# Two transformer blocks on one core: the second block's gates from un-normed tiles, its last two HGRN levels from buffers of their own

## What is computed

```python
x = rmsnorm(x_lat, final_norm)                    # end of block one
xn = rmsnorm_2(x, norm_mix)                       # start of block two
proj = xn @ w_in + b_in                           # h_q, h_f_fwd, h_f_bwd, h_i, h_g, m_q, m_k, m_v, m_o, 16 gates
q_h = silu(h_q);  lf = log_sigmoid(h_f) per direction;  k = 1 - exp(lf)
# HGRN2 per head and direction:  S_t = diag(f_t) S_{t-1} + k_t v_t^T,  o_t = S_t^T q_t
```

## Time and profile before

| | us |
|---|---|
| median of 3 runs | 1798.23 |
| lowest, highest | 1798.11, 1799.66 |
| profiled execution | 1801.54 |
| its span, first to last instruction | 1799.8 |
| PE busy | 1711.2 |
| VectorE busy | 959.0 |
| ScalarE busy | 702.5 |
| GpSimd busy | 138.6 |

### The profile page before, as it was taken

The page is one execution under the profiler, slowest core; times in us unless marked ns, Lnnn a source line. Parts: engine busy times, 40 slices in busy tenths (PEclk is TensorE's granted clock), DMA queues, the critical chain, the costliest instruction groups (busy, mean ns, idle before and its releaser), DMA issues.

```text
span 1799.8 us, 18749 instructions
## 1 busy us (share of the span) xinstructions
PE 1711.2 (95%) x7182; PEld 1289.3 (72%) x7182; DVE 959.0 (53%) x1325; ACT 702.5 (39%) x1024; POOL 138.6 (8%) x150
## 2 busy tenths in 40 slices
PE   7999988989999999999898998989998999999997
PEld 1478755355788888888687877558875688888886
DVE  5867576265454433442568779575533353434343
ACT  2631354312344312334464556865433331313141
POOL 0312000014300000003000000213000100000001
PEclk9999999999999999999899999999999999999999
DMA  9334113401313224213232121334311213232221
GB/s 325 109 116 164 59 48 106 174 37 47 94 48 102 94 86 138 95 59 105 103 119 81 47 59 36 110 121 164 128 59 47 90 53 107 107 106 99 93 93 47
DMA packets 113237, 174.43 MB, mean 97 GB/s; under 512 B 3788, under 2 KB 56524, under 8 KB 112717
## 3 DMA queue, kind: packets, MB, share of 16 engines
q1 hardware_dynamic: 109404, 160.76, 26.2%
q0 software_dynamic: 3760, 12.72, 2.2%
HBM read 169.00 MB, written 4.46 MB: 96 GB/s over the span
## 4 chain that ended last, share of the span: by engine, by line
PE 82%; DVE 7%; ACT 5%; issue 3%; DMA 1%; POOL 1%; SPq 0%; DVEq 0%; ACTq 0%; POOLq 0%
PE bank L833 15%; PE bank L834 15%; PE bank L835 15%; PE bank L866 6%; PE bank L867 6%; PE bank L871 5%; PE bank L891 3%; PE bank L1077 2%; PE bank L940 2%; PE bank L1090 1%; PE bank L1020 1%; PE bank L1032 1%; PE bank L1357 1%; PE bank L1388 1%; PE bank L1207 1%
## 5 line engine op out<-in xcount | busy, mean ns | idle before, releaser
L2945 POOL TENSOR_TENSOR arena<-arena 128x512 f32<-128x512 f32 (+1 forms) x56 | 74.1, 1329 | 981.4 <-ACT arena L1483 977.6
L835 PE MATMUL bank<-hx_hi,weight_slots_lo 128*128 128x512 f32 x320 | 125.7, 393 | 0.0
L1452 ACT ACTIVATE weights_hi<-weight_slots 128x2048 fp32r<-128x2048 f32 (+2 forms) x46 | 77.0, 1725 | 122.2 <-DMA weight_slots<-in_ffn_w_down 65.4
L2089 ACT ACTIVATE weights_hi<-weight_slots 128x2048 fp32r<-128x2048 f32 x30 | 55.8, 1909 | 162.9 <-DMA weight_slots<-in_w_up 108.7
L2902 DVE TENSOR_TENSOR weight_slots_lo<-weight_slots,weights_hi 128x2048 fp32r<-128x2048 f32 x30 | 67.4, 2288 | 87.1 <-ACT weights_hi L2089 87.1
L834 PE MATMUL bank<-xn_lo,weights_hi 128*128 128x512 f32 x288 | 112.0, 389 | 0.0
L1438 ACT ACTIVATE arena<-bank 128x512 f32<-128x512 f32 (+3 forms) x110 | 54.8, 537 | 138.0 <-PE bank L835 50.4
L833 PE MATMUL bank<-sq_hi,weights_hi 128*128 128x512 f32 x256 | 99.6, 389 | 0.0
L834 PE MATMUL bank<-sq_lo,weights_hi 128*128 128x512 f32 x256 | 99.6, 389 | 0.0
L835 PE MATMUL bank<-sq_hi,weight_slots_lo 128*128 128x512 f32 x256 | 99.6, 389 | 0.0
L2139 DVE TENSOR_TENSOR weight_slots_lo<-weight_slots,weights_hi 128x2048 fp32r<-128x2048 f32 (+2 forms) x36 | 70.2, 1990 | 29.8 <-ACT weights_hi L1452 29.8
(11 more groups left out here) (422 smaller groups left out, 4138.4 us busy)
## 6 DMA issues: line engine op xcount, KB each, us to landing
weight_slots<-in_w_in SPq DMA_DIRECT2D x24, 1024.0 KB, 7.0
weight_slots<-in_ffn_w_up SPq DMA_DIRECT2D x22, 1024.0 KB, 6.5
weight_slots<-in_w_up SPq DMA_DIRECT2D x16, 1024.0 KB, 6.5
weight_slots<-in_w_down SPq DMA_DIRECT2D x16, 1024.0 KB, 6.3
weight_slots<-in_w_mod SPq DMA_DIRECT2D x14, 1024.0 KB, 7.7
arena<-in_w_mod POOLq DMA_DIRECT2D x32, 256.0 KB, 3.3
weight_slots<-in_w_out SPq DMA_DIRECT2D x8, 1024.0 KB, 7.6
weight_slots<-in_w_xkv SPq DMA_DIRECT2D x8, 1024.0 KB, 7.4
```

What stands on the lines that cost most here:

```text
L835: return mm(ps, ll, rh, start=False, stop=stop)
L1452: A(high_half(kind, n, i), W[:, s_, a:b], ACT.Copy).then_inc(w_hi, 1)
L2089: A(W_hi[:, s % 2, a:b], W[:, s % 2, a:b], ACT.Copy).then_inc(w_hi, 1)
L2945: G.tensor_tensor(acc, acc, sq[i % 2][:, 0:width], ALU.add).then_inc(sq_added, 1)
```

## The change

1. **Un-normed gates and hq.** ScalarE copies xg_hi = x * gain_mix2 right behind each tile's squares, and VectorE makes xg_lo (`gained_low`). PE does the gate and hq products with these; the norm sums stand between tiles k = 2 and k = 3. VectorE multiplies the five results with rstd on the way out of PSUM, then ScalarE adds biases and takes the Silu in place. hx is still made, for ff and the later projections. Slab down,7 is split by ScalarE behind the squares of three tiles, and slab in2,1 before hx's high parts; VectorE splits both halves of in2,0 before it adds up tile 7.
2. **Slab waits by halves.** Gates and hq start at half 0 of in2,0 and wait for half 1 at k = 4; hi, mv and mq (all that 3 + n < RING lets through) do the same with theirs.
3. **Work moved between the f and b projections.** Own keys of hp 0 (behind n = 6), the subtraction that makes Gc (per tile instead of over 2048 columns), x's normalising (behind n = 0 and 2; the store x_rest follows it, now behind the transfer of in2,2). The references of the far levels are made at place (1, 3); the mask cast moves behind level 2's exponents.
4. **Far exponents in ScalarE.** For levels 256 and 512, `exponents` is no longer called. ScalarE computes exp(ref - F) with the reference as its bias, in pieces of 128 columns, and the other halves in larger pieces (10 activations for 256, 14 for 512).
5. **Buffers of their own.** For hp 1 the far levels use the parts of Fc, Gc, kf and kb that belonged to hp 0 (`far_buffers`), and are made at places (4, 3) and (5, 0). The gate scans wait for (1,512)'s scores, since they write there.

```diff
+FAR_AT = {(4, 3): 256, (5, 0): 512}
+REFERENCES = (1, 3)
...
+OWN_KEYS = 6
+GAINED_LOW = {2: (0, 1), 3: (2,), 5: (3, 4), 6: (5, 6)}
+MID_TILES = {0: range(0, 4), 2: range(4, 8)}
 IN2_SPLIT = 6
 
 
-HIGH_HOMES = {3: (54, 74), 4: (58, 70), 5: (54, 50)}
+HIGH_HOMES = {1: (32, 40), 3: (54, 74), 4: (58, 70), 5: (54, 50)}
...
+        xg_hi = parts("xg_hi", 54, 8)
+        xg_lo = [parts("xg_lo_26", 26, 6)[:, k, :] for k in range(6)] + [parts("xg_lo_14", 14, 2)[:, k, :] for k in range(2)]
...
+        def far_buffers(lev):
+
+            return [t[:, 0:1024] for t in ((Fc, Gc) if lev == 256 else (kf, kb))]
+
+        def near_count(hp, lev):
+
+            return len(LEVELS) * hp + LEVELS.index(lev) + 1
...
+            slab("in2", 2, io["w_in_2"], 1024)
             sp.wait_ge(normed, sum(norms["norm_mid"]))
             sp.dma_start(x_rest, x).then_inc(sem("x_away"), 16)
-            slab("in2", 2, io["w_in_2"], 1024)
...
-            norm_sum("norm_mid")
-            norm_sum("norm_mix2")
-
             pe.wait_ge(sem("wgate_lo"), 1)
-            w = split_slab("in2", 0)
+            pe.wait_ge(w_lo, 2 * split_no["in2", 0] + 1)
+            w = [v.rearrange("p (k c) -> p k c", k=KD) for v in (high("in2", 0), low("in2", 0))]
             gates, *banks = [open_bank(name) for name in ["gates"] + [f"hq_{m}" for m in range(HC)]]
             cols = [slice(P * m, P * m + P) for m in range(HC)]
             for k in range(KD):
-
-                pe.wait_ge(x_hi, operand_no["hx", k] + 1)
-                mm(gates[:], wgate_hi[:, k, :], hx_hi[:, k, :], start=k == 0, stop=False)
-                mm(gates[:], wgate_lo[:, k, :], hx_hi[:, k, :], start=False, stop=False)
+                if k == 4:
+                    pe.wait_ge(w_lo, 2 * split_no["in2", 0] + 2)
+                if k == 3:
+                    norm_sum("norm_mid")
+                    norm_sum("norm_mix2")
+
+                pe.wait_ge(x_hi, operand_no["xg", k] + 1)
+                mm(gates[:], wgate_hi[:, k, :], xg_hi[:, k, :], start=k == 0, stop=False)
+                mm(gates[:], wgate_lo[:, k, :], xg_hi[:, k, :], start=False, stop=False)
                 for c, ps in zip(cols, banks):
-                    mm(ps[:], w[0][:, k, c], hx_hi[:, k, :], start=k == 0, stop=False)
-                    mm(ps[:], w[1][:, k, c], hx_hi[:, k, :], start=False, stop=False)
+                    mm(ps[:], w[0][:, k, c], xg_hi[:, k, :], start=k == 0, stop=False)
+                    mm(ps[:], w[1][:, k, c], xg_hi[:, k, :], start=False, stop=False)
...
+                if hp and lev > P:
+                    pe.wait_ge(sem("far_decay_A"), 1 + (lev == 512))
+                    pe.wait_ge(sem("far_B_ready"), 1 + (lev == 512))
+                    A, B = far_buffers(lev)
+                elif lev:
...
-                    pe.wait_ge(w_lo, 2 * split_no["in2", 3 + n] + 2)
+                    pe.wait_ge(w_lo, 2 * split_no["in2", 3 + n] + 1)
...
+                    if 3 + n < RING and k == KD // 2:
+                        pe.wait_ge(w_lo, 2 * split_no["in2", 3 + n] + 2)
...
+                if k == 3:
+                    split_w("down", 7)
                 evicted(act, f"down_{KD + k}")
                 square_tile("norm_mid", k, x[:, k, :])
                 square_tile("norm_mix2", k, x[:, k, :], scale=pc("final_norm", k))
+                if k == 0:
+                    act.wait_ge(sem("gain_mix2"), 1)
+                A(xg_hi[:, k, :], x[:, k, :], ACT.Copy, scale=gain_mix2[:, k:k + 1]).then_inc(x_hi, 1)
...
+            def far_exp(hp, lev, dst, left, right, dl, dr):
+
+                o, l, r = (v.rearrange("p (h j t) -> p h j t", h=2, j=NT)
+                           for v in (dst, left[:, 1024 * hp:1024 * hp + 1024], right[:, 1024 * hp:1024 * hp + 1024]))
+
+                def from_ref(h, j, row):
+                    c = 4 * (2 * hp + h) + j
+                    return A(o[:, h, j, :], l[:, h, j, :], ACT.Exp, scale=-1.0, bias=refs[:, row, c:c + 1])
...
+                if lev == 256:
+                    for h in range(2):
+                        for j in (0, 2):
+                            from_ref(h, j, dl)
+                    return A(o[:, :, 1:4:2, :], r[:, :, 1:4:2, :], ACT.Exp)
+                for h in range(2):
+                    for j in (0, 1):
+                        from_ref(h, j, dl + 2)
+                A(o[:, :, 2, :], r[:, :, 2, :], ACT.Exp)
+                for h in range(2):
+                    c = 4 * (2 * hp + h) + 2
+                    ins = A(o[:, h, 3, :], r[:, h, 3, :], ACT.Exp, bias=refs[:, dr, c:c + 1])
+                return ins
...
+                        far_exp(hp, lev, A_, kf, kb, 0, 1).then_inc(sem("far_decay_A"), 1)
+                        far_exp(hp, lev, B_, Gc, Fc, 1, 0).then_inc(sem("far_decay_B"), 1)
...
+            def gained_low(k):
+
+                dve.wait_ge(x_hi, operand_no["xg", k] + 1)
+                V.scalar_tensor_tensor(xg_lo[k], x[:, k, :], gain_mix2[:, k:k + 1], xg_hi[:, k, :].bitcast(F32),
+                                       ALU.mult, ALU.subtract).then_inc(x_lo, 1)
...
-                    if half and m >= KD - 2:
-                        split_w("in2", 0, (m - KD + 2,))
+                    if half and m == 2:
+                        dve.wait_ge(sem("gain_mix2"), 1)
+                    for k in GAINED_LOW.get(m, ()) if half else ():
+                        evicted(dve, f"{kind}_{KD + k}")
+                        gained_low(k)
+                    if half and m == KD - 2:
+                        split_w("in2", 0)
...
+            for name, dst in [("gates", zg)] + [(f"hq_{m}", q2[:, 512 * m:512 * m + 512]) for m in range(HC)]:
+                ps = full(dve, name)
+                free(V.tensor_tensor(dst, ps[:], rstd[:], ALU.mult), name)
...
+                    if d:
+
+                        link(ins)
+                        link(V.tensor_copy(refs[:, 1, NT * m:NT * m + NT], C[:, c].rearrange("p (j t) -> p j t", t=P)[:, :, P - 1]))
+                        ins = V.tensor_tensor(C[:, c], C[:, c], lf[:, c], ALU.subtract)
+                    ins.then_inc(sem("lf_ready"), 1)
...
+                    if n in MID_TILES:
+                        for k in MID_TILES[n]:
+                            V.scalar_tensor_tensor(x[:, k, :], x[:, k, :], pc("final_norm", k), r_mid, ALU.mult, ALU.mult).then_inc(normed, 1)
+                    if n == OWN_KEYS:
+                        own_keys(0)
...
-                if lev == 0:
-
-                    c = slice(1024 * hp, 1024 * hp + 1024)
-                    dve.wait_ge(sem("own_keys"), 2 * hp + 2)
-                    V.tensor_tensor(A_, A_, B_, ALU.add).then_inc(sem("keys_added"), 1)
-                    link(V.tensor_tensor(kf[:, c], Fc[:, c], kf[:, c], ALU.subtract))
-                    link(V.tensor_tensor(kb[:, c], Gc[:, c], kb[:, c], ALU.add))
-                    return
...
+                if hp and lev > P:
+                    dve.wait_ge(sem("far_decay_B"), 1 + (lev == 512))
+                    B_ = far_buffers(lev)[1]
+                    V.tensor_tensor(B_, B_, q2[:, 1024 * hp:1024 * hp + 1024], ALU.mult).then_inc(sem("far_B_ready"), 1)
...
-                        if step_after(*step):
+                        if step_after(*step) and step_after(*step)[1] <= P:
...
+            done(dve, "lv_3_512_1")
```

155 lines of the change are left out of this document (84 added, 71 removed).

## The result

| | before | changed |
|---|---|---|
| median, us | 1798.95 (4 runs) | 1780.55 (4 runs) |
| lowest, highest | 1798.11, 1800.41 | 1780.27, 1781.00 |
| profiled execution | 1801.54 | 1781.00 |
| its span | 1799.8 | 1779.2 |

The ratio is 0.9897, 95% interval 0.988 to 0.9914: 18.4 us by the medians, 20.6 by the two spans. The forecast was 23.0 less, at 1775.2; 1780.55 lies in its range of 1770 to 1784.

The account below looks back on a forecast made before the run. TensorE, busy 95% of the span, was taken as the bound, so gains lie in its rests and slow clock. 11.1 + 6.5 + 5.4 = 23.0 us off the profiled 1801.5 gives 1778.5, less 3.3 to the median: 1775.2, range 1770 to 1784.

Parts of the forecast that it names:

- The front: Last down product to ff_0: un-normed gates and hq, norm sums between tiles 2 and 3, start ff_0 11.1 us earlier.
- The start of the level loop: First levels to mv_0: work moved between fb projections removes waits (4.9) and slow clock (1.6), 6.5 us.
- the one on the store: SyncE's queue: x_rest ahead of slab in2,3, both there near 922, ScalarE wants it at 920.5; pushes VectorE by 2 us.
- the 11 us: Behind the last fb projection: VectorE is through with fb_3 about 11 us behind PE, the store's 2 us included.
- the rest at mv_0: Start of the level loop: 3.1 us before the change, taken as gone; its presence would show the forecast wrong.
- Rival A: First levels: VectorE stays the bound, mv_0's rest and slow clock return (3.1 + 1.6), 1779.9; chance 0.17.
- The last levels: Second heads' last two levels: rest before (1,512) 1.85 instead of 4.33, slow clock gone (2.9), together 5.4 us.
- The named queue on VectorE: Before (1,512)'s last multiply: low part (1.22), (1,128)'s mask copies (1.32), multiply (1.21); PE rests 1.85.
- Rival C: Before (1,512): the clock falls at the remaining 1.85 us rest, sum 2.9 us smaller, 1778.1; chance 0.12.
- B: Before (1,512): the last rest doesn't shrink, 24 small activations precede (1,128); 5.4 back, 1780.6; chance 0.12.
- E: Front: gates don't start early, copies delay GpSimd's adds and the slab split; 5 us back, 1780.2; chance 0.05.
- F (a level's round trip): Level loop: a level's round trip becomes the bound, 9.9 against PE's 7.24, 2.7 lost at 14 levels, 1812; chance 0.02.

Follow-up runs that it names:

- x3: Against the changed kernel, far levels 256 and 512 of heads 2, 3 go into alternating buffers A and B, not their own: median 1785.06 us, ratio to before 0.9917.

## Why the prediction was right, and where it was off

**1. The front, 11.1 forecast, 11.7 measured.** From D to ff_0 it was 42.95 and is 31.29. The first gate product came 0.3 us late behind the last down product, as forecast (0.15 of it is listed as rest), and the 120 products took what their rows said. The 0.6 is a price that was too high: the forecast has 0.51 for half of a norm sum, half of the 1.02 in which a pair is listed, but a pair starts every 0.86 us (860.13, 860.99), so the eight halves took 3.4 and not 4.1. The chain to the first hx_lo stayed hidden. ff_0 starts 31.3 behind D; the forecast's 31.6 counts from 854.1, 0.2 behind D, and so is 31.8 by this measure. (Half 1 of the slab is needed 40 products and the sums in, not 36 products; nothing hangs on it.) With the operands and the place of the sums undone, the front costs 14.6.

**2. The start of the level loop, 6.5 forecast, 5.2 measured** (between ff_0 and the rest before mk's slab column, at 1077.61 before and 1059.61 after: 18.0 of gain there, less 12.8 at ff_0). The clock stayed at 1.00, the rests did not all go. The step that failed is the one on the store: "both are there near 922 ... That pushes VectorE by 2 us, which is in the 11 above". The transfer landed at 923.6, ScalarE waited 4.24, and the 11 us had no room for it: PE rested at 928, 954 and 959. The last of these is the rest at mv_0 that the forecast had named as a sign of being wrong, at 0.38 us and without the slow clock. With the store behind the slab, 2.3 more came, so the place holds 7.5, one more than the term. The likely reason is that rests were priced at their listed length, where each cost 0.3 more in the run with the store moved; for the three rests of the kernel before this was not measured. Rival A did not come: 2.3 were lost of its 4.7, and by the late slab, not by VectorE's work. And the credit was given wrongly: moving own keys gave nothing, and the waits by halves carry 2.8 of this place (and 2.2 of the front).

**3. The last levels, 5.4 forecast, 5.3 measured.** T to (1,512) went as worked out: a rest of 1.81 (1.85 forecast), 3.69 at full clock instead of 6.49, 14 activations in 4.2. The named queue on VectorE was the whole of the rest. The missing row for an activation with a reference as bias was rightly taken as 0.29: four start in 1.17.

**The clock.** The row said that a rest of 2.56 had left the clock at 1.00 and that the 2.32 had not, and the forecast sided with the first for the 1.85. It held: 1.00 behind 1.81, and 0.50 behind 3.90 in x3. Rival C did not come at its place, but its mechanism did, at the very rest of 2.56 that had been the witness against it: 0.57 behind it in the changed kernel. The step that failed is the one that isn't there: the forecast took everything behind H as unchanged, and the clock there cost 2.8 us in one profile of the changed kernel and 0.2 in the other. The Trainium skill (TensorE: Matmul & The Clock Gate, What's actually happening) says that the check of the array's activity runs on by itself and doesn't start anew with a kernel, so that the point of a transition varies from run to run. Two profiles of one kernel of which one has clock 0.50 from 1348.7 on and the other 1.00 agree with that; that it alone decides was not shown.

**The sum.** 11.7 + 5.2 + 5.3 = 22.2 against 23.0. That this is so close is in part luck: the front came 0.6 better and the level loop 1.3 worse than forecast. The forecast's 1775.2 is 5.35 below the median measured. Of that, 0.8 is the three terms; 1.6 is what the profiles differ by outside D to H (2.8 lost, 1.2 won); and 2.9 is that the forecast took the distance from profiled execution to median, 3.3 in the kernel before, for the changed one too, where it is 0.45. Its base was low: 26 further executions of the kernel before took 1797.81 to 1803.99, so the profiled 1801.54 was an ordinary one and the median of three, 1798.23, a low one. So 0.8 lies in the terms, and the rest in how single executions differ and in whatever the clock loses behind H on average. The measured 1780.55 also falls on the prices of rivals A (1779.9), B (1780.6) and E (1780.2), but by the timelines none of the three happened. F (a level's round trip) had no sign: between mv_0 and T PE rests 0.58, 0.84 and 0.19 us, as it did before the change.

## What to carry to other kernels

When an operand waits for a norm, multiply with the un-normed one and scale the result; but give the norm's own sum a place in the middle of that work, or its wait comes back (4.8 us here). After moving work beside TensorE, look at what each moved transfer now stands in front of on its queue: a 2 MB store in front of a slab cost 2.3 of the 7.5 us of a place. Measure a change of a per cent between two landmarks of one profile rather than by medians alone: here the first repeats to 0.1 us, the second to 1 or 2.

## What was not expected of the hardware

- Behind the same rest of 2.56 us eight products took 2.87 us in nine profiles and 4.57 in five (clock 1.00, and 0.57 or 0.58, where the windows were read), and of one kernel's two profiles one fell to 0.50 behind a rest of 1.89 and the other stayed at 1.00 (eight products in 5.15 and 3.67 us soon after). There no rest near it is longer than 1.9 us.
- A short rest of TensorE costs more than its listed length: 0.29, 0.72 and 0.38 were worth 0.59, 0.96 and 0.68 when they went, and 1.81 was worth 2.04. About 0.16 of each short one is the tail of the product before it.
